# The row scales of the first norm go through DRAM instead of through TensorE

## The chip, the cores and the metric

The kernel runs on one core of a Trainium2 chip. The time is device microseconds of one launch. The kernel before takes 1110.6 us, the median of three runs (1110.36 to 1110.89).

## The reference

One hybrid decoder layer over 256 positions of width 1024, all in 32-bit floats: a mixer (8 mLSTM heads and 8 block-attention heads of 64), a mixture of 32 experts with 4 chosen for each position, and a gated per-layer embedding. What the change touches is the first norm and the combined projection behind it, with the gate columns of the mLSTM heads:

```
h = x * rsqrt(mean(x * x) + 1e-6) * mix_norm_g          # 256 rows, 1024 wide
u = h @ w_in                                            # 3600 columns, split among the head groups
ml_qk, ml_v, ml_o, ml_i, ml_f, mb_q, mb_k, mb_v = split(u)
i_pre = ml_i + igate_b ;  f_pre = ml_f + fgate_b        # 8 columns each: the gates
q_b = rmsnorm(mb_q, q_norm_g) / 8 ;  k_b = rmsnorm(mb_k, k_norm_g)
```

Behind it stand the two mixers, `x += mixed @ w_out`, the experts (`w_gate_up` of 32 x 1024 x 2048 and `w_down` of 32 x 1024 x 1024, read in full), and the embedding with its gate `w_ple_gate`.

## The kernel before, in words

The rows are two tiles of 128 positions (`tt` 0 and 1). `x` lies in the tile named arena, and TensorE transposes it so that the 1024 inputs lie on the partitions, in eight slices (`k`). The transposed slices are multiplied by `mix_norm_g` and stored in `rawT` (named big in the profile): ScalarE writes slices 0 to 3 (`raw_half`, L1787), VectorE slices 4 to 7 (L1329). `rawT` still lacks the norm's factor, one number for each position, the row scale `rstd`. ScalarE sums the squares and takes the root (`row_root`, L1794), VectorE takes the reciprocal (`rstd`, L1317) into two columns of `stat`, one number per partition.

The projection runs as 18 jobs, each of eight steps over `k` into one of two PSUM banks (hu 0 and 1). Jobs 0 and 1 are the attention queries of the two row tiles. They take `rawT`, without the scale, and the scale is applied afterwards, on the rows. All later jobs take `hT`, which is `rawT` times the row scale. There the positions lie along the free dimension, so the scale is needed as a row of 256 numbers on all 128 partitions. Before the change two matmuls make that row: `stat`'s column, broadcast, against the identity (L776) into PSUM bank hu 3. `scaled(tt)` (L1334) makes one half of `hT` with it.

The gates are computed apart: eight small matmuls (L783) over all of `rawT` give partial sums `gpart`, which VectorE copies and multiplies by the same row (L1346, L1348), and two matmuls (L794) add the partial sums. VectorE then runs ten gate steps on 8 partitions (L1392 to L1403), with an exponential and a logarithm on ScalarE between them. `normed_half(i)` (L1354) divides job i's result by its heads' norms. It stands before the gate steps for job 0 and behind them for job 1.

The order on each engine is that in which the code is written, and every engine runs its own list. Semaphores join the lists. TensorE's list at the start is: transposes, job 0, the two row matmuls, the gates' partial sums, eight small transposes of parameter rows (L788), two steps of job 1, the gate sums, six steps of job 1, job 2 (L714), four transposes of job 0's normalised result (L807, which wait for the tenth gate step), four small ones (L816), job 3. Job 2 waits for both halves of `hT` and for job 0's bank (`normed_half(0)`), job 3 for `normed_half(1)`.

The weights come on SyncE's DMA queue into a ring of eleven slots of up to 2 MB. The next transfer into a slot is issued when TensorE has finished with the slot's content. The small parameters come on ScalarE's queue (q10 in the profile). One such round trip through DRAM exists already: the row maxima of the mLSTM heads are stored by ScalarE (L1831) and loaded on all partitions by SyncE (L490).

Of the kernel before, what the change touches and what calls it, by code (L numbers as in the profile page):

```python
# [15 lines left out]
F32 = mybir.dt.float32  # L16
I32 = mybir.dt.int32
U32 = mybir.dt.uint32
ALU = mybir.AluOpType
# [3 lines left out]
P = 128  # L23
# [10 lines left out]
def hybrid_layer(nc, x, p, mix_norm_g, w_in, conv_w, conv_b, igate_b, fgate_b, mlstm_head_g, q_norm_g,  # L34
                 k_norm_g, w_out, ffn_norm_g, w_router, b_router, w_gate_up, b_gate_up, w_down, b_down,
                 ple_norm_g, w_ple_gate, w_ple_proj, out):
    S, D = x.shape[1:]
# [3 lines left out]
    K = D // P  # L41
    TT = S // P
# [58 lines left out]
    with ctx:  # L101
        def sb(name, shape, dt=F32):
            return ctx.enter_context(nc.sbuf_tensor(name, shape, dt))

        def sem(name):
            return ctx.enter_context(nc.semaphore(name))


        hu = ctx.enter_context(nc.psum_tensor("hu", [P, 4, NB], F32))
# [5 lines left out]
        ident = sb("ident", [P, P])  # L115
# [16 lines left out]
        early = arena[:, TT * D:]  # L132

        stat = sb("stat", [P, 64])
# [41 lines left out]
        gpart = num_xg[:, 0:S]  # L176
# [33 lines left out]

        zeros = early[:, 0:P]
        sq_junk = early[:, 2 * S:2 * S + D]

        const_ready = sem("const_ready")
        zero_ready = sem("zero_ready")
# [6 lines left out]
        first_loaded = sem("first_loaded")  # L222
        second_loaded = sem("second_loaded")
        third_loaded = sem("third_loaded")
        rowb_ps = sem("rowb_ps")
        small_loaded = sem("small_loaded")
        late_loaded = sem("late_loaded")
        wo_ps = sem("wo_ps")
# [7 lines left out]
        gpart_ready = sem("gpart_ready")  # L236
# [5 lines left out]
        rstd_ready = sem("rstd_ready")  # L242
# [111 lines left out]
        def slot(n, width, parts):  # L354

            return ring[:, PRE_SLOT[n], 0:parts * width].rearrange("p (k n) -> p k n", n=width)
# [43 lines left out]
        def final_slot(c, width, parts):  # L400

            return ring[:, SLOT_OF[POSITIONS + c], 0:parts * width].rearrange("p (k n) -> p k n", n=width)

        def last_of_chunk(j):
            return j + 1 == JOBS or JOB_CHUNK[j + 1] != JOB_CHUNK[j]

        def done_job(j, ins):

            ins.then_inc(chunk_done if last_of_chunk(j) else job_ps, 1)
# [30 lines left out]
        def fin_bank(q, lo, hi):  # L440

            return (po[:, 1, :] if lo else LAST_BANKS[q])[:, lo:hi]
# [7 lines left out]
            return buf[:, q // HALVES, (q % HALVES) * NB:(q % HALVES + 1) * NB]  # L450

        xt_d = nc.dram_tensor("xt_scratch", (P, TT, D), F32).ap()
        negm_d = nc.dram_tensor("negm_scratch", (H, S), F32).ap()

        block = ctx.enter_context(nc.Block())
# [230 lines left out]
        def _(pe):  # L686
            mm = nc.tensor.matmul
# [65 lines left out]
            def raw_job(tt, ks):  # L753

                for k in ks:
                    last = mm(hu[:, tt, :], rawT[:, k, tt * P:(tt + 1) * P], slot(0, NB, K)[:, k, :], start=(k == 0),  # L756
                              stop=(k == K - 1), skip_group_check=True)
                return last
# [12 lines left out]
            raw_transposes(1)  # L771
            wait_chunk(pe, 0)
            done_job(0, raw_job(0, range(6, K)))
            for tt in range(TT):
                pe.wait_ge(rstd_ready, tt + 1)
                last = mm(hu[:, 3, tt * P:(tt + 1) * P], stat[:, 16 + tt:17 + tt].to_broadcast([P, P]), ident[:], start=True, stop=True)  # L776
            last.then_inc(rowb_ps, 1)
            pe.wait_ge(hT_act, 8)
            pe.wait_ge(hT_dve, 2)
            pe.wait_ge(small_loaded, 16 * 3)  # L780
            for k in range(K):
                c = 32 * (k % 4)
                last = mm(aux[c:c + 32, 1, 0:S], w_if[:, k, :], rawT[:, k, :], start=(k < 4), stop=(k >= 4),  # L783
                          skip_group_check=True)
            last.then_inc(gpart_ps, 1)
            pe.wait_ge(rows_loaded, 16 * 8)
            for k in range(K):
                last = tr(hu[:, 2, k * ROWS:(k + 1) * ROWS], rows[:, k * P:(k + 1) * P], ident[0:ROWS, 0:ROWS])  # L788
            last.then_inc(cols_ps, 1)
            raw_job(1, range(0, 2))  # L790
            pe.wait_ge(gpart_ready, 2)
            pe.wait_ge(const_ready, 6)
            for gi in range(2):
                last = mm(aux[0:H, 0, gi * S:(gi + 1) * S], sel_part[:, gi * H:(gi + 1) * H], gpart, start=True, stop=True)  # L794
            last.then_inc(gate_ps, 1)
            done_job(1, raw_job(1, range(2, K)))

            def norm_transposes(i):

# [14 lines left out]
            for c, src in enumerate((arow, negmt)):  # L814
                for tt in range(TT):
                    last = tr(hu[:, 2 + c, tt * H:(tt + 1) * H], src[:, tt * P:(tt + 1) * P], ident[0:H, 0:H])  # L816
# [228 lines left out]
            def scatter_expert(q, e, bank, more=False):  # L1045

                tt, n = divmod(q, HALVES)
                r = slice(n * SLOTS, (n + 1) * SLOTS)
                return mm(bank, ghotT[r, e, tt * P:(tt + 1) * P], out_s[e][r, :], start=(e == 0), stop=(e == 1 and not more))  # L1049
# [80 lines left out]
            with pe.Fori(0, npass) as ps:  # L1130
# [151 lines left out]
                for tt in range(TT):  # L1282
                    for n in range(HALVES):
                        last = scatter_expert(HALVES * tt + n, 1, LAST_BANKS[HALVES * tt + n])
# [9 lines left out]
            for q, lo, hi in FIN:  # L1294
                tt, n = divmod(q, HALVES)
                for k in range(K):
# [4 lines left out]
                    elif n == 0:  # L1301
                        pe.wait_ge(hT_dve, 2 + 4 * tt + k - 3)
                    last = mm(fin_bank(q, lo, hi), x3T[:, k, tt * P:(tt + 1) * P],  # L1303
                              final_slot(k // 4, D, 4)[:, k % 4, n * NB + lo:n * NB + hi],
                              start=(k == 0), stop=(k == K - 1))
# [6 lines left out]
        def _(dve):  # L1312
            v = nc.vector
# [20 lines left out]
            def scaled(tt):  # L1334

                r = slice(tt * P, (tt + 1) * P)
                dve.wait_ge(hT_act, 4 * tt + 4)
                dve.wait_ge(hT_dve, tt + 1)
                v.tensor_tensor(hT[:, :, r], rawT[:, :, r],
                                hu[:, 3, r].rearrange("p (o t) -> p o t", o=1).to_broadcast([P, K, P]), ALU.mult)\  # L1340
                 .then_inc(xs_ready, 1)

            dve.wait_ge(rowb_ps, 1)
            scaled(0)
            dve.wait_ge(gpart_ps, 1)
            v.tensor_copy(gpart, aux[:, 1, 0:S]).then_inc(gpart_ready, 1)  # L1346
            dve.wait_ge(gpart_ready, 1)
            v.tensor_tensor(gpart, gpart, hu[:, 3, 0:S], ALU.mult).then_inc(gpart_ready, 1)  # L1348
            dve.wait_ge(cols_ps, 1)
            v.tensor_copy(cols[:].rearrange("p k r -> p (k r)"), hu[:, 2, 0:K * ROWS]).then_inc(cols_ready, 1)  # L1350
            scaled(1)
            dve.wait_ge(cols_ready, 1)

            def normed_half(i):  # L1354

                ss = small[:, 0:H]
                dve.wait_ge(sq_ready, i + 1)
                v.tensor_reduce(ss, sq_junk[:, i % 2 * W:(i % 2 + 1) * W].rearrange("p (h d) -> p h d", h=H), AX.X, ALU.add).then_inc(nstat, 1)
                dve.wait_ge(nroot, i + 1)
                v.reciprocal(small[:, 3 * H:4 * H], small[:, 2 * H:3 * H]).then_inc(nstat, 1)  # L1360
                dve.wait_ge(nstat, 2 * i + 2)
                if i >= 2:
                    dve.wait_ge(normT_ps, i - 1)
                out = normed[:, i % 2, :].rearrange("p (h d) -> p h d", h=H)
                q = hu[:, i % 2, :].rearrange("p (h d) -> p h d", h=H)
                inv = small[:, 3 * H:4 * H].rearrange("p (h o) -> p h o", o=1).to_broadcast([P, H, DH])
                if i < TT:
                    v.scalar_tensor_tensor(out=out, in0=q, scalar=stat[:, 16 + i:17 + i], in1=inv, op0=ALU.mult, op1=ALU.mult)\
                     .then_inc(normed_ready, 1)
                else:  # L1370
                    v.tensor_tensor(out, q, inv, ALU.mult).then_inc(normed_ready, 1)
# [13 lines left out]
            n = [0]  # L1385
# [378 lines left out]
        def _(act):  # L1764
            a = nc.scalar

            def root(i, src, wait):

                if wait:
                    act.wait_ge(sum_ready, i - 1)  # L1770
                a.activation(stat[:, 8 + i:9 + i], src, ACT.Sqrt, scale=1.0 / D, bias=eps_t[:]).then_inc(root_ready, 1)
# [15 lines left out]
            def raw_half(tt):  # L1787

                act.wait_ge(xT_ps, 2 * tt + 1)
                for k in range(4):  # L1790
                    a.activation(rawT[:, k, tt * P:(tt + 1) * P], QUAD_BANKS[2 * tt][:, k * P:(k + 1) * P], ACT.Copy,
                                 scale=g_mix[:, k:k + 1]).then_inc(hT_act, 1)

            def row_root(tt):  # L1794

                act.wait_ge(x_loaded[tt], 16)
                if tt:
                    act.wait_ge(ss_ready, tt)
                a.activation(sq_junk[:], xt[:, tt, :], ACT.Square, accum_out=stat[:, tt:tt + 1]).then_inc(ss_ready, 1)
                act.wait_ge(ss_ready, tt + 1)  # L1800
                root(tt, stat[:, tt:tt + 1], False)
# [2 lines left out]
            raw_half(0)  # L1804
            row_root(0)
            row_root(1)
            raw_half(1)
            act.wait_ge(root_warm, 1)

            for i in range(4):  # L1810
# [248 lines left out]
            for i, (q, lo, hi) in enumerate(FIN):  # L2059
                tt = q // HALVES  # L2060
# [27 lines left out]
```

## Time and profile before

| | before |
|---|---|
| median of 3 runs | 1110.6 us |
| the profiled execution | 1110.49 us |
| its span | 1108.7 us |
| TensorE busy | 1071.0 us, 97% |
| weights and the rest moved | 431.89 MB, 390 GB/s on average |

A row of the timeline gives the start, the duration, the engine (PE is TensorE, DVE VectorE, ACT ScalarE, SPq and ACTq the issuing of a DMA by SyncE and ScalarE), the line, the operation, the tiles written and read, the shapes, and in brackets how long the engine had been idle and for what. The chain of waits is followed back from the last instruction. A row of it is a stretch that the end depended on. "PEclk" is the granted TensorE clock, 1.00 being 2.4 GHz and 0.50 being 1.2 GHz.

### The profile page before, as it was taken

To read this page: it belongs to the slowest core of one execution; us is meant where nothing else is said; L and a number is where in the kernel's file an instruction comes from. 1 tells how busy PE (TensorE), PEld (TensorE's weight loads), DVE (VectorE), ACT (ScalarE), POOL (GpSimd) and SP (SyncE) were. 2 spreads that over 40 slices of the span, in tenths; PEclk is the share of its full clock that TensorE was granted. 3 is DMA by queue.
4 is the path that set the end of the run, shared out by engine and by line. 5 is a ranking of instruction groups with operands and counts; after the bars stand their busy time and mean duration, and the time that the engine had idled before them with its cause. 6 is when DMAs were issued, how large, how long until landed. Compare 5 with 4: busy or idle time off the path is not lost.

```text
span 1108.7 us, 12040 instructions
## 1 busy us (share of the span) xinstructions
PE 1071.0 (97%) x5136; PEld 445.1 (40%) x5136; DVE 258.7 (23%) x534; ACT 144.6 (13%) x283; POOL 16.3 (1%) x40
## 2 busy tenths in 40 slices
PE   9999999999999999999999899998989999999898
PEld 5485563434343434343434232333333344423234
DVE  4274242231121212121212121111212021202122
ACT  4134341100000000000000000000000100000022
POOL 1001100000000000000000000000000000000000
PEclk9999999999999999999999999999999999999999
DMA  9943589999999999999999999999999999999971
GB/s 347 361 168 123 240 343 387 426 426 430 427 426 429 427 427 427 427 429 425 428 429 426 429 429 426 429 427 427 427 427 425 429 427 426 429 428 426 427 324 38
DMA packets 43004, 431.89 MB, mean 390 GB/s; under 512 B 6231, under 2 KB 6751, under 8 KB 17606
## 3 DMA queue, kind: packets, MB, share of 16 engines
q1 hardware_dynamic: 42736, 431.07, 93.0%
q8 instruction: 41, 0.67, 0.2%
q14 instruction: 13, 0.11, 0.0%
q10 hardware_dynamic: 214, 0.04, 0.0%
HBM read 430.04 MB, written 1.06 MB: 389 GB/s over the span
## 4 chain that ended last, share of the span: by engine, by line
PE 66%; DMA 33%; DVE 0%; issue 0%; ACT 0%; SPq 0%; DVEq 0%; ACTq 0%
PE hu L1094 23%; DMA ring<-in_w_gate_up 23%; PE po L1124 14%; DMA ring<-in_w_down 6%; PE aux L1041 5%; PE hu L714 5%; DMA ring<-in_w_ple_gate 3%; PE hu L720 3%; PE aux L1049 2%; PE hu L1086 2%; PE hu L730 2%; PE hu L756 1%; PE po L1101 1%; PE aux L1303 1%; PE aux L1074 1%; PE po L1303 1%
## 5 line engine op out<-in xcount | busy, mean ns | idle before, releaser
L1094 PE MATMUL hu<-ring,num_xg 128*64 128x512 f32 x1920 | 433.2, 598 | 24.4 <-DMA ring<-in_w_gate_up 24.4
L1094 PEld LDWEIGHTS hu<-ring,num_xg 128*64 128x64 f32 x1920 | 131.9, 137 | 305.9 <-issue 258.7
L1124 PE MATMUL po<-ring,arena 128*64 128x512 f32 x976 | 217.8, 596 | 6.5 <-DMA ring<-in_w_down 6.5
L1124 PEld LDWEIGHTS po<-ring,arena 128*64 128x64 f32 x976 | 67.4, 137 | 152.7 <-issue 136.8
L1669 DVE TENSOR_SCALAR arena<-hu 128x512 f32<-128x512 f32 x31 | 21.4, 692 | 431.9 <-PE hu L1094 431.9
L1645 DVE TENSOR_TENSOR arena<-arena,aux 128x512 f32<-128x512 f32 x58 | 37.3, 684 | 133.2 <-PE aux L1049 121.4
L1041 PEld LDWEIGHTS aux<-num_xg,big 128*128 128x128 f32 x512 | 58.4, 192 | 13.0 <-issue 13.0
L1041 PE MATMUL aux<-num_xg,big 128*128 128x128 f32 x512 | 61.4, 278 | 0.0
L714 PE MATMUL hu<-ring 128*128 128x512 f32 x128 | 56.7, 596 | 0.0
L1992 ACT ACTIVATE hu<-arena 128x512 f32<-128x512 f32 x31 | 18.6, 601 | 250.7 <-DVE arena L1669 250.7
L1658 DVE TENSOR_SCALAR arena<-iota_s,posm,gates 128x128 f32<-128x128 f32 x64 | 17.9, 343 | 118.3 <-PE po L1124 115.3
L2008 ACT COPY arena<-po 128x512 f32<-128x512 f32 x16 | 9.4, 586 | 220.7 <-PE po L1114 220.7
L1049 PE MATMUL aux<-num_xg,arena 64*128 64x512 f32 x124 | 35.0, 641 | 0.1
L714 PEld LDWEIGHTS hu<-ring 128*128 128x128 f32 x128 | 23.8, 190 | 27.7 <-issue 27.4
L1086 PE MATMUL hu<-bias,sel_part 32*64 32x512 f32 x256 | 34.8, 612 | 0.0
L1049 PE MATMUL aux<-arena 64*128 64x512 f32 x124 | 31.8, 589 | 0.0
L1996 ACT COPY arena<-po 128x512 f32<-128x512 f32 x31 | 18.2, 586 | 90.3 <-PE po L1101 90.3
L720 PE MATMUL hu<-ring 128*128 128x256 f32 x128 | 29.5, 385 | 0.0
L1094 PE MATMUL hu<-ring,arena 128*64 128x512 f32 x128 | 28.1, 594 | 0.1
L730 PE MATMUL hu<-ring 128*128 128x512 f32 (+1 forms) x64 | 25.8, 543 | 0.0
L720 PEld LDWEIGHTS hu<-ring 128*128 128x128 f32 x128 | 23.7, 190 | 4.8 <-DVE ring L1444 1.0
L2000 ACT COPY num_xg<-po 128x512 f32<-128x512 f32 x16 | 9.4, 586 | 114.9 <-PE po L1124 114.9
(276 smaller groups left out, 606.8 us busy)
## 6 DMA issues: line engine op xcount, KB each, us to landing
ring<-in_w_gate_up SPq DMA_DIRECT2D x125, 2048.0 KB, 37.3
ring<-in_w_down SPq DMA_DIRECT2D x60, 2048.0 KB, 38.0
ring<-in_w_in SPq DMA_DIRECT2D x6, 2048.0 KB, 17.1
ring<-in_w_gate_up SPq DMA_DIRECT2D x6, 1024.0 KB, 7.9
ring<-in_w_out SPq DMA_DIRECT2D x2, 2048.0 KB, 11.7
ring<-in_w_down SPq DMA_DIRECT2D x4, 1024.0 KB, 37.1
ring<-in_w_ple_gate SPq DMA_DIRECT2D x2, 2048.0 KB, 33.6
ring<-in_w_in SPq DMA_DIRECT2D x4, 512.0 KB, 6.6
```

The lines of the kernel that those rows point to most:

```text
L714: last = mm(bank, hT[:, k, tt * P:(tt + 1) * P], slot(n, NB, K)[:, k, :], start=(k == 0), stop=(k == K - 1))
L720: last = mm(bank[:, 0:S], slot(n, NB, K)[:, k, ct * P:(ct + 1) * P], hT[:, k, :], start=(k == 0), stop=(k == K - 1))
L730: last = mm(bank[:, lo:hi], mixT[:, k, tt * P:(tt + 1) * P], slot(n, D, 4)[:, k % 4, b * NB + lo:b * NB + hi], start=(k == 4), stop=(k == 3))
L1041: last = mm(bank[:, (k % 4) * P:(k % 4 + 1) * P], h2[:, tt, k * P:(k + 1) * P], onehot[:, tt, :, :].rearrange("p e s -> p (e s)"), start=( ...
L1049: return mm(bank, ghotT[r, e, tt * P:(tt + 1) * P], out_s[e][r, :], start=(e == 0), stop=(e == 1 and not more))
L1086: mm(hu[n * SLOTS:(n + 1) * SLOTS, 2 * e + b, :], expert_rows(b, expert), bias[32 * b:32 * b + E, n * NB:(n + 1) * NB], start=first, stop= ...
L1094: last = mm(hu[n * SLOTS:(n + 1) * SLOTS, 2 * e + b, :], rows_of[:, k, e * SLOTS:(e + 1) * SLOTS], w[:, o:o + NB], start=first, stop=(k == ...
L1124: last = mm(bank[n * SLOTS:(n + 1) * SLOTS, :], actT[:, f, h * SLOTS:(h + 1) * SLOTS], w[:, o:o + NB], start=(h == 0 and f == 0), stop=(h ...
L1303: last = mm(fin_bank(q, lo, hi), x3T[:, k, tt * P:(tt + 1) * P], final_slot(k // 4, D, 4)[:, k % 4, n * NB + lo:n * NB + hi], start=(k == ...
L1645: v.tensor_tensor(quad(xt, q), quad(xt, q), banks[q], ALU.add).then_inc(y_done, 1)
L1669: v.tensor_scalar(glu, hu[:, 2 * e, :], LIMIT, None, ALU.min).then_inc(glu_ready, 1)
L1992: a.activation(hu[:, 2 * e, :], gated(2 * pair + e), ACT.Sigmoid, scale=ALPHA).then_inc(sig_ready, 1)
```

## The change

The two matmuls that made the row are gone. ScalarE stores the two columns of scales as 2 x 128 numbers in a DRAM tensor, and loads the 256 numbers back on all 128 partitions into `scales`, a part of arena. The stores stand before `raw_half(1)` in ScalarE's list and wait for both reciprocals. The load stands behind it and waits for both stores to have landed. In TensorE's list the gate sums move from behind two steps of job 1 to behind four. In VectorE's list the copies out of PSUM come first, then the gates' product, then both halves of `hT`.

```diff
             done_job(0, raw_job(0, range(6, K)))
-            for tt in range(TT):
-                pe.wait_ge(rstd_ready, tt + 1)
-                last = mm(hu[:, 3, tt * P:(tt + 1) * P], stat[:, 16 + tt:17 + tt].to_broadcast([P, P]), ident[:], start=True, stop=True)
-            last.then_inc(rowb_ps, 1)
             pe.wait_ge(hT_act, 8)
 ...
-            raw_job(1, range(0, 2))
+            raw_job(1, range(0, 4))
             pe.wait_ge(gpart_ready, 2)
 ...
-            done_job(1, raw_job(1, range(2, K)))
+            done_job(1, raw_job(1, range(4, K)))
 ...
                 v.tensor_tensor(hT[:, :, r], rawT[:, :, r],
-                                hu[:, 3, r].rearrange("p (o t) -> p o t", o=1).to_broadcast([P, K, P]), ALU.mult)\
+                                scales[:, r].rearrange("p (o t) -> p o t", o=1).to_broadcast([P, K, P]), ALU.mult)\
                  .then_inc(xs_ready, 1)
 
-            dve.wait_ge(rowb_ps, 1)
-            scaled(0)
             dve.wait_ge(gpart_ps, 1)
             v.tensor_copy(gpart, aux[:, 1, 0:S]).then_inc(gpart_ready, 1)
-            dve.wait_ge(gpart_ready, 1)
-            v.tensor_tensor(gpart, gpart, hu[:, 3, 0:S], ALU.mult).then_inc(gpart_ready, 1)
             dve.wait_ge(cols_ps, 1)
             v.tensor_copy(cols[:].rearrange("p k r -> p (k r)"), hu[:, 2, 0:K * ROWS]).then_inc(cols_ready, 1)
-            scaled(1)
             dve.wait_ge(cols_ready, 1)
+            dve.wait_ge(scales_loaded, 16)
+            dve.wait_ge(gpart_ready, 1)
+            v.tensor_tensor(gpart, gpart, scales, ALU.mult).then_inc(gpart_ready, 1)
+            for tt in range(TT):
+                scaled(tt)
 ...
             row_root(1)
+            act.wait_ge(rstd_ready, TT)
+            for tt in range(TT):
+                act.dma_start(scale_d[tt:tt + 1, :].rearrange("o p -> p o"), stat[:, 16 + tt:17 + tt]).then_inc(scales_stored, 16)
             raw_half(1)
+            act.wait_ge(scales_stored, 16 * TT)
+            act.dma_start(scales, scale_d.rearrange("t p -> (t p)").rearrange("(o n) -> o n", o=1).to_broadcast([P, S]))\
+               .then_inc(scales_loaded, 16)
```

TensorE's list before, from job 0 to job 2 (L756 are the steps of jobs 0 and 1, L776 the row matmuls, L783 the gates' partial sums, L794 the gate sums):

```order
L749 MATMUL po<-ident,arena 128x128 x8
L756 MATMUL hu<-ring,big 128x512 x2
L776 MATMUL hu<-ident,stat 128x128 x2
L783 MATMUL aux<-big,ring 32x256 x8
L788 MATMUL hu<-ident,ring 128x10 x8
L756 MATMUL hu<-ring,big 128x512 x2
L794 MATMUL aux<-num_xg,sel_part 8x256 x2
L756 MATMUL hu<-ring,big 128x512 x6
L714 MATMUL hu<-ring 128x512 x8
```

The same place after the change, three to nine lines further down in the file:

```order
L752 MATMUL po<-ident,arena 128x128 x8
L759 MATMUL hu<-ring,big 128x512 x2
L782 MATMUL aux<-big,ring 32x256 x8
L787 MATMUL hu<-ident,ring 128x10 x8
L759 MATMUL hu<-ring,big 128x512 x4
L793 MATMUL aux<-num_xg,sel_part 8x256 x2
L759 MATMUL hu<-ring,big 128x512 x4
L717 MATMUL hu<-ring 128x512 x8
```

The row matmuls are gone, and two steps of job 1 have moved ahead of the gate sums.

ScalarE's list before, from the second root on (`raw_half(1)`, then the squares of job 0 and their root):

```order
L1799 ACTIVATE arena,stat<-arena 128x1024
L1771 ACTIVATE stat<-stat,eps_t 128x1
L1791 ACTIVATE big<-po,g_mix 128x128 x4
L1819 ACTIVATE arena<-hu,stat 128x512
L1823 ACTIVATE small<-small,eps_t 128x8
```

The same place after:

```order
L1798 ACTIVATE arena,stat<-arena 128x1024
L1770 ACTIVATE stat<-stat,eps_t 128x1
L1808 DMA scale_scratch<-stat 128x1 x2
L1790 ACTIVATE big<-po,g_mix 128x128 x4
L1811 DMA arena<-scale_scratch 128x256
L1824 ACTIVATE arena<-hu,stat 128x512
L1828 ACTIVATE small<-small,eps_t 128x8
```

Two stores stand ahead of `raw_half(1)` now, and a load ahead of the squares of job 0.

VectorE's list before, from the second reciprocal to the first gate step (L1339 are the halves of `hT`):

```order
L1320 RECIPROCAL stat<-stat 128x1
L1339 TENSOR_TENSOR ring<-big,hu 128x8x128
L1346 COPY num_xg<-aux 128x256
L1348 TENSOR_TENSOR num_xg<-num_xg,hu 128x256
L1350 COPY cols<-hu 128x80
L1339 TENSOR_TENSOR ring<-big,hu 128x8x128
L1358 TENSOR_REDUCE small<-arena 128x8
L1360 RECIPROCAL small<-small 128x8
L1368 SCALAR_TENSOR_TENSOR ring<-hu,stat,small 128x512
L1392 TENSOR_SCALAR ring<-aux,fg_bias 8x256
```

The same place after:

```order
L1319 RECIPROCAL stat<-stat 128x1
L1343 COPY num_xg<-aux 128x256
L1345 COPY cols<-hu 128x80
L1349 TENSOR_TENSOR num_xg<-num_xg,arena 128x256
L1338 TENSOR_TENSOR ring<-big,arena 128x8x128 x2
L1357 TENSOR_REDUCE small<-arena 128x8
L1359 RECIPROCAL small<-small 128x8
L1367 SCALAR_TENSOR_TENSOR ring<-hu,stat,small 128x512
L1391 TENSOR_SCALAR ring<-aux,fg_bias 8x256
```

Everything from the gates' product on now stands behind the load of the scales.

## Rows read from the trace of the kernel before

**Rows 1.** The page: engines, then the span in 40 slices.
```profile
PE 1071.0 (97%) x5136; PEld 445.1 (40%) x5136; DVE 258.7 (23%) x534; ACT 144.6 (13%) x283; POOL 16.3 (1%) x40
PEclk9999999999999999999999999999999999999999
DMA  9943589999999999999999999999999999999971
```

**Rows 2.** The chain of waits: start, duration, what it was.
```profile
12.52 1.72 PE hu L756 x4
14.69 1.00 PE aux L783 x16
16.28 1.91 PE hu L756 x4
18.20 0.96 PE aux L794 x4
19.16 5.35 PE hu L756 x12
24.51 6.87 PE hu L714 x16
32.15 7.06 PE hu L714 x16
...
543.18 39.89 DMA ring<-in_w_gate_up
```

**Rows 3.** Stretches: bounds, length, busy PE PEld DVE ACT POOL, clock, DMA share, GB/s.
```profile
12.00:16.00 4.00, 4.00 (x35) 2.34 (x34) 1.98 (x4) 1.83 (x5) 0.00 (x0) 1.00 1.05 387
142.00:144.00 2.00, 2.00 (x10) 1.55 (x10) 0.69 (x1) 0.16 (x1) 1.60 (x2) 1.00 0.12 45
157.00:160.00 3.00, 3.00 (x19) 2.67 (x18) 1.65 (x8) 2.69 (x4) 0.00 (x0) 1.00 0.57 186
200.00:543.00 343.00, 342.93 (x1728) 131.94 (x1726) 74.32 (x129) 26.58 (x45) 0.00 (x0) 1.00 1.01 428
```

**Rows 4.** The timeline around the row matmuls.
```profile
12.11 1.14 ACT L1791 ACTIVATE big<-po,g_mix 128x128 f32<-128x128 f32 x4 [0.23 <-PE po L749]
13.24 0.15 DVE L1320 RECIPROCAL stat<-stat 128x1 f32<-128x1 f32 x1
```

**Rows 5.** DMAs on ScalarE's queue: two issues, and its packets in 44.8:45.5.
```profile
0.80 0.42 ACTq L1773 DMA_DIRECT2D g_mix<-in_mix_norm_g  x1
...
41.07 0.28 ACTq L1831 DMA_DIRECT2D negm_scratch<-arena  x1
...
q10 hardware_dynamic: 16, 0.01, 4.0%
```

**Rows 6.** Packets on SyncE's queue in 12:16, and DMAs to landing (last number).
```profile
q1 hardware_dynamic: 755, 1.55, 105.0%
...
g_mix<-in_mix_norm_g ACTq DMA_DIRECT2D x1, 4.0 KB, 4.1
ring<-in_mlstm_head_g SPq DMA_DIRECT2D x1, 256.0 KB, 9.1
```

**Rows 7.** The timeline of VectorE from the gates' product to `normed_half(1)`.
```profile
16.37 0.42 DVE L1348 TENSOR_TENSOR num_xg<-num_xg,hu 128x256 f32<-128x256 f32 x1
16.71 0.23 DVE L1350 COPY cols<-hu 128x80 f32<-128x80 f32 x1
16.86 1.21 DVE L1339 TENSOR_TENSOR ring<-big,hu 128x1024 f32<-128x1024 f32 x1
17.99 0.68 DVE L1358 TENSOR_REDUCE small<-arena 128x8 f32<-128x512 f32 x1
...
27.88 0.75 DVE L1368 SCALAR_TENSOR_TENSOR ring<-hu,stat,small 128x512 f32<-128x512 f32 x1
```

**Rows 8.** Stretches around a fall of the clock, columns as in rows 3.
```profile
809.80:813.40 3.60, 3.60 (x16) 1.05 (x16) 0.00 (x0) 0.00 (x0) 0.00 (x0) 1.00 1.03 437
813.45:815.90 2.45, 0.00 (x1) 0.00 (x0) 0.00 (x0) 0.00 (x0) 0.00 (x0) 1.00 1.01 421
816.80:820.20 3.40, 3.40 (x10) 0.96 (x8) 0.00 (x0) 0.00 (x0) 0.00 (x0) 0.50 0.98 419
```

**Rows 9.** A shorter idle stretch in the timeline, and what followed in the chain.
```profile
583.11 1.08 PE L1094 MATMUL hu<-ring,num_xg 128*64 128x512 f32 x4 [1.24 <-DMA ring<-in_w_gate_up]
...
583.11 3.65 PE hu L1094 x16
```

More of the change, by code:

```diff
@@ L212, in hybrid_layer @@
         sq_junk = early[:, 2 * S:2 * S + D]
+        scales = early[:, 6 * S:7 * S]
         const_ready = sem("const_ready")
@@ L224, in hybrid_layer @@
         third_loaded = sem("third_loaded")
-        rowb_ps = sem("rowb_ps")
+        scales_stored = sem("scales_stored")
+        scales_loaded = sem("scales_loaded")
         small_loaded = sem("small_loaded")
@@ L452, in hybrid_layer @@
         xt_d = nc.dram_tensor("xt_scratch", (P, TT, D), F32).ap()
+        scale_d = nc.dram_tensor("scale_scratch", (TT, P), F32).ap()
         negm_d = nc.dram_tensor("negm_scratch", (H, S), F32).ap()
```

## The prediction

> **What bounds the kernel now.** I read the page first: TensorE is busy 97% of the span and the DMA engines nearly all of it from the fifth slice on [rows 1]. Both are candidates, so the place decides. The chain of waits says that from 12 us to 543 us the end depends on TensorE, and that at 543 us it changes over to a transfer of weights, 39.89 us from issue to landing [rows 2]. Around the change TensorE has no gap at all: 4.00 us busy of the 4.00 from 12 us on [rows 3]. So whatever TensorE waits there is added to its list in full.
>
> Does that reach the end, since behind 543 us the transfers set the pace? The stream of weights has full engines from 200 us (share 1.01), but not at 142 us (0.12) and not at 157 us (0.57) [rows 3]. There it waits for ring slots that TensorE has to free, while TensorE is busy throughout. A later TensorE frees them later, the stream starts its unbroken run later, and the whole rest moves by the same amount. I pass every microsecond of the front on to the end, one to one.
>
> **The change, part by part.**
>
> *The two row matmuls go.* In the chain there are 0.45 us between the end of job 0 (12.52 + 1.72 = 14.24) and the partial sums (14.69) [rows 2]. That is a gain of 0.45 us, if the partial sums can start at 14.24.
>
> *They cannot, because `raw_half(1)` is late.* The partial sums read all of `rawT`, and before, ScalarE had its four slices written at 12.11 + 1.14 = 13.25 [rows 4], well hidden. Now ScalarE first waits for the second reciprocal, which ends at 13.24 + 0.15 = 13.39 [rows 4], and issues two DMAs. The nearest row for one of 128 partitions is 0.42 us of issuing [rows 5]. With 0.1 us for the semaphore: stores issued at 13.5 and 13.92, ScalarE free at 14.35, `raw_half(1)` done at 15.5. The partial sums start near 15.6 instead of 14.69, so this alone turns the gain of 0.45 into a loss of about 0.9 us. They and the small transposes take 16.28 - 14.69 = 1.59, the four steps of job 1 twice the 1.92 of two (18.20 - 16.28) [rows 2]: TensorE stands before the gate sums at 21.0.
>
> *When do the scales arrive?* Call it T. Two transfers in a row, each waited for. The best row is the store that the kernel already makes on the same queue, beside the same stream of weights: issued at 41.07, all of its 16 packets (8 rows and what closes them) moved between 44.8 and 45.5 [rows 5]. So some 4.3 us from issue to landing, nearly all of it before the first byte. Ours has 128 pieces, eight on each of 16 DMA engines. If each takes its turn with one packet of the weights, of which 755 went by in 4 us on 16 engines [rows 6], 4 x 16 / 755 = 0.085 us each, seven more pieces cost 0.6 us, and the other store's pieces stand in between. I take 5.1 us from the second issue: 13.92 + 5.1 = 19.0. The load is issued at 19.1. It has the same 4.3 us, 0.6 us for eight turns, and its pieces are 1 KB each, about half of those 0.085 us, 0.35 us for eight: 5.3 us, so T = 24.4. From below: g_mix, 128 pieces of 32 bytes issued into an empty chip, took 4.1 us to land [rows 6]; 13.92 + 4.1 + 0.1 + 4.1 gives T = 22.2. A gain from a transfer is not possible, since the scales were there at once before. From above: a load on all partitions, of 256 KB on the other queue, took 9.1 us [rows 6], which with a store of 5.1 gives T = 28.2. I take 24.4, since its rows are of the same queue under the same traffic.
>
> *What waits for T on VectorE.* The gates' product, both halves of `hT`, `normed_half(0)`, the ten gate steps and `normed_half(1)` are all behind it. From the spacing of the starts: product 16.71 - 16.37 = 0.34, each half of `hT` 17.99 - 16.86 = 1.13 [rows 7]. So the reduction of `normed_half(0)` starts at T + 0.1 + 0.34 + 2.26 = T + 2.7. From there to the end of `normed_half(1)` it was 27.88 + 0.75 - 17.99 = 10.64 us [rows 7], through ScalarE's roots, exponential and logarithm, which keep their place in that sequence. That is T + 13.35, and job 3 can start at T + 13.45.
>
> *What waits for T on TensorE.* The gate sums start at T + 0.65 (semaphore, 0.42 for the product, semaphore, weight load). For T = 24.4 that is 25.05, so TensorE idles for 4 us. Then 0.96 for the sums, four steps at 5.35 x 4 / 6 = 3.57, and 32.15 - 24.51 = 7.64 from the start of job 2 to that of job 3 [rows 2]: T + 12.8. VectorE's path is the later one, at T + 13.45. The two moved steps of job 1 cover 2 x 0.96 = 1.9 us of the wait, and the calculation has them in it. Job 2 itself needs both halves and job 0's bank, T + 4.75, and TensorE comes at T + 5.2. The transposes need the tenth gate step, about 2.1 us before T + 13.35, that is T + 11.3, and TensorE comes at T + 12.05.
>
> *The clock.* Behind 2.45 us in which TensorE did nothing, the granted clock was 0.50 (1.2 of 2.4 GHz) for 3.40 us of work [rows 8], and behind 1.24 us of idling another stretch kept its rate: 16 matmuls in 3.65 us [rows 9], against 3.60 at full clock and 10 in 3.40 in the slow stretch [rows 8]. Our gap is 4 us, so I expect one such stretch here. It costs half of 3.4, 1.7 us, on TensorE's path: T + 14.5, which is then the later of the two.
>
> *The rest.* ScalarE stands at the store's wait until 19.1, and the squares of job 0 behind it come near 20 instead of 14.33; their reader on VectorE is at T + 2.7 anyway. GpSimd's and SyncE's later waits for the gate steps feed work far behind. The scales read from arena instead of PSUM I price at nothing: both products run one element per cycle by their durations (1.21 us for 1024) [rows 7], and a change of 0.1 us there either way is inside the range. The three DMAs move 128 KB and 1 KB, some 0.35 us of the engines at 387 GB/s [rows 3], in front of weights whose first unmet need is at 543 us [rows 2]: nothing.
>
> *The sum.* Before, job 3 started at 32.15 [rows 2]. After: 24.4 + 14.5 = 38.9. That is 6.75 us later, or 24.4 + 13.45 - 32.15 = 5.7 us if the clock stays up. The profiled execution took 1110.49 us (0.1 below the median), so I forecast 1110.5 + 6.75 = 1117.25, rounded to 1117.2.
>
> **The rivals.**
>
> *Quick round trip.* If T is below about 19.7, VectorE's path (T + 13.45) is behind TensorE's own, which stands before the gate sums at 21.0 and reaches job 3 at 21.0 + 0.96 + 3.57 + 7.64 = 33.2. Then only the late `raw_half(1)` counts: +1.0 us, 1111.5. It needs both transfers within about 2.8 us of issue. For it: 1 KB and less to move. Against: the shortest landing in the rows is 4.1 us [rows 6]. The Trainium skill (DMA: Bandwidth & Descriptors, Anatomy of one DMA) gives 2.0 us of fixed cost for each DMA and next to nothing for so few bytes, which by that page puts T near 18.9 and the result in this rival; no row of this trace shows a transfer that short.
>
> *Not slower at all.* The same with the store's issue costing ScalarE next to nothing, so that `raw_half(1)` is done by 14.2: it would need issues of 0.1 us or less each against the 0.28 and 0.42 of the rows [rows 5]. Then the 0.45 us of the row matmuls are won: 1110.0. It decides from T below 18.2.
>
> *The delay is swallowed.* TensorE's first wait for weights is at 543 us [rows 2]. If the stream did not start later, TensorE could be 7 us late in front and lose nothing: 1110.5. Against it speak the two stretches in which the stream has nothing to do [rows 3].
>
> *A slow load or slow stores.* 4-byte writes to DRAM do not occur in this trace. If the pair takes as long as the upper bound, T = 28.2, then 28.2 + 14.5 - 32.15 = 10.55 us: 1121.0.
>
> **Chances.** The forecast's own case (T from 22.2 to 26.5) 73%, the slow transfers 13%, quick round trip 7%, swallowed delay 5%, not slower at all 2%. The range goes from T = 22.2 without a fall of the clock (3.5 us: 1114.0), half a microsecond taken off for the estimates in it, to just above the upper bound: 1113.5 to 1121.5. About 0.2%, 2.2 us, is what a measurement of this kernel can tell from no change. Slower by more than that: 0.86, the first two cases. Within: 0.11, quick, swallowed and not slower in most of their cases. Faster: 0.03.
>
> **What would show it.** In the profile after: two stores issued near 13.5 on ScalarE's queue, `raw_half(1)` starting near 14.4; the load issued near 19; the gates' product on VectorE starting near 24.5; an idle TensorE before the gate sums, about 4 us, where there was none; a stretch at clock 0.50 behind it; job 3 starting near 39; and the same lateness of 6 to 7 us at the first expert matmul and at the end. It is wrong if the gate sums do not wait (quick round trip), or if the late start of job 3 is not found again at the end (swallowed).

## The result and the profile after

| | before | after |
|---|---|---|
| median of 6 runs each | 1110.48 us | 1127.35 us |
| range of the runs | 1109.78 to 1110.91 | 1126.65 to 1128.99 |
| ratio, 95% interval | | 1.0151 (1.0141 to 1.0161) |
| span of the profiled execution | 1108.7 us | 1124.9 us |

The kernel is slower by 16.9 us. Forecast were 6.7, with a range that ended at 1121.5. The direction was right, the size less than half of what came.

The chain of waits of the changed kernel says where it went (start, duration, what). It answers to [rows 2]:

```profile
13.73 12.58 DMA scale_scratch<-stat
26.33 7.13 DMA arena<-scale_scratch
34.02 1.88 PE aux L793 x4
35.90 4.89 PE hu L759 x8
40.79 6.87 PE hu L717 x16
48.44 7.06 PE hu L717 x16
```

The second store alone took 12.58 us, the load 7.13. Job 3 (the last row, L717 is L714 of before) starts at 48.44 instead of 32.15, 16.3 us late. The span has grown by 16.2. So nearly all of it arose before job 3, and nearly all of it reached the end.

The timeline around it (start, duration, engine, line, in brackets the idle time before). These rows answer to [rows 4, 7]:

```profile
13.33 0.85 ACTq L1808 DMA_DIRECT2D scale_scratch<-stat  x2
14.23 1.14 ACT L1790 ACTIVATE big<-po,g_mix 128x128 f32<-128x128 f32 x4 [2.52 <-DVE stat L1319]
15.43 0.85 PE L782 MATMUL aux<-big,ring 128*32 128x256 f32 x12 [1.27 <-ACT big L1790]
...
33.54 0.43 DVE L1349 TENSOR_TENSOR num_xg<-num_xg,arena 128x256 f32<-128x256 f32 x1 [16.16 <-DMA arena<-scale_scratch]
34.02 1.88 PE L793 MATMUL aux<-num_xg,sel_part 128*8 128x256 f32 x4 [13.30 <-DVE num_xg L1349]
```

ScalarE issues both stores and is late for `raw_half(1)`, and TensorE waits 1.27 us for it, as forecast. The last two rows are the trip through DRAM: VectorE had nothing to do for 16.16 us, TensorE for 13.30.

Stretches of the changed kernel, columns as in [rows 3]:

```profile
12.00:16.00 4.00, 2.73 (x20) 1.25 (x23) 0.76 (x2) 1.14 (x4) 0.00 (x0) 1.00 1.05 386
19.00:21.00 2.00, 1.72 (x5) 0.42 (x3) 0.00 (x0) 0.00 (x0) 0.00 (x0) 1.00 1.04 27
20.80:34.00 13.20, 0.00 (x0) 0.00 (x0) 0.46 (x2) 0.69 (x1) 0.00 (x0) 0.65 0.97 216
34.10:38.30 4.20, 4.20 (x7) 1.47 (x8) 3.80 (x6) 1.42 (x2) 0.00 (x0) 0.50 1.05 400
158.00:161.00 3.00, 3.00 (x13) 2.19 (x12) 1.30 (x4) 0.30 (x1) 1.62 (x2) 1.00 0.18 76
216.00:560.00 344.00, 343.94 (x1730) 132.35 (x1728) 74.75 (x131) 27.08 (x46) 0.00 (x0) 1.00 1.01 427
```

Three things stand here. From 19 to 21 us the DMA engines are as busy as ever (1.04) and move 27 GB/s instead of 387: the stores hinder the weights too. Behind the gap TensorE works at the lower clock, a granted clock of 0.50. And 16 us further down the stream of weights has the same hole as before (0.18 at 158 us) and the same unbroken run behind it: the whole rest has moved.

The packets of SyncE's queue between 18 and 22 us (number, MB, share of 16 engines) answer to [rows 6]:

```profile
q1 hardware_dynamic: 145, 0.30, 113.5%
```

That is 1.135 x 16 x 4 / 145 = 0.50 us for a packet of the weights, of some 2 KB. Before it was 1.050 x 16 x 4 / 755 = 0.089 us.

### The profile page after: what moved, and what is told of

Same layout as the page of the kernel before. It is cut to its first block, busy times and chain, and to the rows that moved or that the text cites. A ratio compares the mean times of both kernels' runs of the same rounds, so it can differ in the third digit from the quotient of the medians.

```text
span 1124.9 us, 12035 instructions
## 1 busy us (share of the span) xinstructions
PE 1071.4 (95%) x5132; PEld 444.6 (40%) x5132; DVE 258.6 (23%) x534; ACT 144.4 (13%) x283; POOL 16.4 (1%) x40
## 4 chain that ended last, share of the span: by engine, by line
PE 65%; DMA 34%; DVE 1%; issue 0%; ACT 0%; SPq 0%; ACTq 0%; DVEq 0%
PE hu L1093 22%; DMA ring<-in_w_gate_up 22%; PE po L1123 14%; DMA ring<-in_w_down 6%; PE aux L1040 5%; PE hu L717 5%; DMA ring<-in_w_ple_gate 3%; PE hu L723 3%; PE aux L1048 2%; PE hu L1085 2%; PE hu L733 2%; DMA scale_scratch<-stat 1%; PE po L1100 1%; PE aux L1302 1%; PE hu L759 1%; PE aux L1073 1%
## 5 line engine op out<-in xcount | busy, mean ns | idle before, releaser
L717 PE MATMUL hu<-ring 128*128 128x512 f32 x128 | 56.7, 596 | 0.0
L717 PEld LDWEIGHTS hu<-ring 128*128 128x128 f32 x128 | 23.8, 190 | 27.7 <-issue 27.4
```

The costliest lines, as they stand in the source:

```text
L717: last = mm(bank, hT[:, k, tt * P:(tt + 1) * P], slot(n, NB, K)[:, k, :], start=(k == 0), stop=(k == K - 1))
```

## The experiments

Theory A, formed on this trace: many 4-byte pieces written side by side into 1 KB of DRAM hinder each other and all that the DMA engines do besides. The rivals are these: any small piece is slow; a store to DRAM under this traffic is slow whatever its shape; the wait and the blocked issues around the stores make them slow; and the new order on VectorE and TensorE costs as well. In the edits below, "..." stands for lines left out, such as the declarations of semaphores and of the DRAM tensor.

### The stores alone

The two stores are added to the kernel before, in the place where the changed kernel has them. Nothing on the path waits for them:

```diff
...
             row_root(1)
+            act.wait_ge(rstd_ready, TT)
+            for tt in range(TT):
+                act.dma_start(scale_d[tt:tt + 1, :].rearrange("o p -> p o"), stat[:, 16 + tt:17 + tt]).then_inc(scales_stored, 16)
             raw_half(1)
...
+            pool.wait_ge(scales_stored, 16 * TT)
+            g.memset(stat[:, 60:61], 0.0)
             pool.wait_ge(gate_step, GATE_STEPS)
```

> The kernel before, with the two stores of 128 x 4 bytes put where the changed kernel has them; nobody on the path waits for them (GpSimd alone does, and then writes one idle column). Theory A, the 4-byte writes to DRAM themselves choke the DMA engines: the weights fall below 100 GB/s for some 5 us from 17 to 24 us, the stores land some 12 us after issue, as in the changed kernel, and the time moves only by the late raw_half(1), +0.8 us. Rival B, the stores are slow because ScalarE then sits in a wait and SyncE in a blocked issue, not by themselves: landing in 5 us, weights undisturbed. Rival C, the disturbance delays the weights enough to cost time by itself: over +3 us with no wait for the scales.

Measured: 1111.99 us beside 1110.86 (1.0008, 0.9998 to 1.0017). Its landing, shortest, median and longest of the two, and a stretch:

```profile
DMA to landing us min/median/max: 12.4/12.7/13.1
```
```profile
19.00:21.00 2.00, 2.00 (x7) 0.76 (x7) 1.60 (x4) 1.35 (x2) 0.00 (x0) 1.00 1.33 21
```

The stores are as slow with ScalarE at work instead of waiting, so that half of rival B falls. The other half, SyncE's blocked issue, is still there: it stands in the kernel before as well (one group of issues takes 21.30 us from 4.64 on, here 28.13), and the next run decides on it. The weights choke just as much (21 GB/s), and the time hardly moves. Up to 60 us the chain of waits of this run holds TensorE alone and no transfer of weights, so these are far enough ahead here, and rival C falls too. What costs is waiting for the stores, not having them.

### The pieces apart

```diff
-        scale_d = nc.dram_tensor("scale_scratch", (TT, P), F32).ap()
+        scale_d = nc.dram_tensor("scale_scratch", (TT, P, 1024), F32).ap()
...
-                act.dma_start(scale_d[tt:tt + 1, :].rearrange("o p -> p o"), stat[:, 16 + tt:17 + tt]).then_inc(scales_stored, 16)
+                act.dma_start(scale_d[tt, :, 0:1], stat[:, 16 + tt:17 + tt], allow_slow_non_contiguous=True).then_inc(scales_stored, 16)
```

> As the run with the stores alone, but each 4-byte piece goes to its own 4 KB of DRAM instead of beside its neighbours. If neighbouring pieces in the same line of memory hinder each other, the landing falls from 12 us to 5 or 6 us and the weights keep about 387 GB/s. If any 4-byte write to DRAM is slow, both stay as with the pieces together.

```profile
DMA to landing us min/median/max: 5.2/5.4/5.7
```
```profile
19.00:21.00 2.00, 2.00 (x8) 0.82 (x8) 1.60 (x4) 1.55 (x2) 0.10 (x1) 1.00 1.05 390
```

The same 256 pieces of 4 bytes, on the same queue at the same moment, land in 5.4 us, and the weights keep 390 GB/s. (Time 1112.1 us, 1.0012, 1.0002 to 1.0021.) SyncE's issue is blocked here for 21.16 us, as in the kernel before, so the rest of rival B falls. It is the neighbourhood, not the size or the number.

How near is too near? The same was run with 64 and with 512 bytes from piece to piece (the last size 16 and 128 instead of 1024), and with pieces of 512 bytes one behind the other:

> As the run with the stores alone, each 4-byte piece 64 bytes from the next. My theory (pieces hinder each other only where they fall into the same small stretch of DRAM) leaves open how long the stretch is. If it is 64 bytes or less: landing near 5.4 us, weights undisturbed, as at 4 KB. If it is longer: landing between 5.4 and 12.7 us with a dip in the weights.

> The same with 512 bytes between pieces. If the stretch is 512 bytes or less: landing near 5.4 us, weights at 385 GB/s. If only the number of pieces per page or bank counts: still slow.

```diff
-                act.dma_start(scale_d[tt, :, 0:1], stat[:, 16 + tt:17 + tt], allow_slow_non_contiguous=True).then_inc(scales_stored, 16)
+                act.dma_start(scale_d[tt], xt[:, tt, 0:P]).then_inc(scales_stored, 16)
```

> The stores alone, with 2 x 128 pieces of 512 bytes (a part of x) in place of 4 bytes, one behind the other in DRAM. If neighbours as such were the trouble, this would be slow too. If it is several partial writes to one stretch: landing near 6 us (more bytes, 128 KB), and no dip beyond the 0.3 us that the bytes take.

The landings, for 64 bytes:

```profile
DMA to landing us min/median/max: 5.5/6.0/6.4
```

for 512 bytes:

```profile
DMA to landing us min/median/max: 5.1/5.4/5.7
```

and for the wide pieces:

```profile
DMA to landing us min/median/max: 5.2/5.5/5.7
```

The weights kept 389 GB/s or more from 19 to 21 us in all three; the times of the one run each were 1111.46, 1111.39 and 1111.55 us. At 64 bytes the trouble is gone but for half a microsecond of landing (and 379 GB/s from 17 to 19 us). So it takes several small pieces within 64 bytes or less. Which smaller stretch decides was not tried.

### To a column on chip

```diff
-                act.dma_start(scale_d[tt:tt + 1, :].rearrange("o p -> p o"), stat[:, 16 + tt:17 + tt]).then_inc(scales_stored, 16)
+                act.dma_start(stat[:, 58 + tt:59 + tt], stat[:, 16 + tt:17 + tt]).then_inc(scales_stored, 16)
```

> As the run with the stores alone, but the same 2 x 128 pieces of 4 bytes go to two idle columns on chip instead of to DRAM. If it is the number of small pieces (reading, descriptors), landing stays near 12 us. If it is writing to DRAM, landing is near 5 us and the weights keep 387 GB/s. Time +0.8 us in both.

Measured: 1112.78 us (1.0017, 1.0008 to 1.0027), and from 19 to 21 us 382 GB/s. The stores stand in the list of DMAs as `stat<-stat`, with the median of the two landings at the end:

```profile
stat<-stat ACTq DMA_DIRECT2D x2, 0.5 KB, 5.7
```

So the same 256 pieces of 4 bytes, side by side in two columns on chip, land in 5.7 us, and the weights do not choke: they had 364 GB/s at the least, from 17 to 19 us. It takes writes to DRAM to make them slow. The run cost 0.8 us more than the one with the stores to DRAM alone; its two issues took 0.53 and 0.61 us instead of 0.36 and 0.45, which makes `raw_half(1)` start later behind them by a third of a microsecond, and the rest is inside the intervals.

### The stores in a quiet stream

The changed kernel, with the weights held back:

```diff
             for n in range(1, len(SECTIONS)):
+                if n == 2:
+                    sp.wait_ge(scales_loaded, 16)
                 load(n, slot(n, NB, K), w_in_k[:, :, SECTIONS[n]:SECTIONS[n] + NB])
...
```

> The changed kernel, with SyncE holding back the weights from the third block on until the scales are loaded, so that the trip meets no other traffic. If the stores are slow by themselves (pieces against each other in DRAM): landing still near 12 us, T near 31. If they are slow only beside the weights: landing 3 to 5 us, T = 21 to 23, and the time falls to +4 to +6 us over the kernel before, unless the held back weights then come late themselves.

Measured: 1119.93 us beside 1110.78 (1.0085, 1.0068 to 1.0102). The chain, the packets of ScalarE's queue from 16.0 to 17.4 us, and a stretch behind them:

```profile
13.85 8.78 DMA scale_scratch<-stat
22.65 4.14 DMA arena<-scale_scratch
q10 hardware_dynamic: 288, 0.00, 11.6%
19.00:21.00 2.00, 1.83 (x5) 0.52 (x3) 0.00 (x0) 0.00 (x0) 0.00 (x0) 1.00 0.00 0
```

All 288 packets of the stores (256 pieces and what closes them) moved between 16.0 and 17.4 us, the first of them beside the last of the weights. From 17.4 to 22.6 nothing moved on any queue. What passes in these 5 us the trace does not show; writes that are not yet confirmed would be one reading. So the stores are slow by themselves (8.78 us), and slower beside the weights (12.58). I had expected either the one or the other; it is both. The load takes 4.14 us in quiet and 7.13 in the changed kernel.

### Two rows of 512 bytes instead of 256 pieces

TensorE first turns the two columns into two rows, and one store takes these to DRAM:

```diff
...
             done_job(0, raw_job(0, range(6, K)))
+            pe.wait_ge(rstd_ready, TT)
+            tr(hu[0:TT, 3, 0:P], stat[:, 16:16 + TT], ident[:]).then_inc(rowb_ps, 1)
...
+            dve.wait_ge(rowb_ps, 1)
+            v.tensor_copy(scales[0:TT, 0:P], hu[0:TT, 3, 0:P]).then_inc(row_copied, 1)
             dve.wait_ge(gpart_ps, 1)
...
-            act.wait_ge(rstd_ready, TT)
-            for tt in range(TT):
-                act.dma_start(scale_d[tt:tt + 1, :].rearrange("o p -> p o"), stat[:, 16 + tt:17 + tt]).then_inc(scales_stored, 16)
             raw_half(1)
-            act.wait_ge(scales_stored, 16 * TT)
+            act.wait_ge(row_copied, 1)
+            act.dma_start(scale_d, scales[0:TT, 0:P]).then_inc(scales_stored, 16)
+            act.wait_ge(scales_stored, 16)
...
```

> The changed kernel, but TensorE first transposes the two columns of scales to two rows (one small matmul), VectorE copies them, and one store of 2 x 512 bytes replaces the two stores of 128 x 4 bytes; raw_half(1) is ahead of it again. If the 4-byte writes are what is slow: landing in some 4.5 us, load issued near 19, scales there at T = 24.5, time T - 17.6 = +6.9 us, 1117.4. If any trip through DRAM under this traffic is slow (12 us for a store): no better than the changed kernel, 1127.

Measured: 1118.0 us beside 1110.78 (1.0069, 1.0053 to 1.0086). The chain:

```profile
14.78 4.30 DMA scale_scratch<-arena
19.10 5.45 DMA arena<-scale_scratch
25.12 1.87 PE aux L797 x4
26.99 4.64 PE hu L761 x8
31.63 6.87 PE hu L719 x16
39.28 7.06 PE hu L719 x16
```

This comes near the forecast's sum: a store of 4.30 us (forecast 4.3 before the surcharge for pieces), a load of 5.45 (5.3), the scales at 24.55 (24.4), job 3 at 39.28 (38.9), the time 7.2 us over before (6.7). That the scales come when forecast is in part chance: this store is issued 0.86 us later than the forecast's second one, and lands in 0.8 us less than the 5.1 of the forecast. A trip through DRAM under this traffic costs about 10 us, and some 9.4 us of the changed kernel's loss went with the shape of its stores (1127.35 - 1118.0; the kernel before had medians of 1110.5 and 1110.8 beside them).

### Half the pieces

One store of 128 x 8 bytes. The scales of the two row tiles then alternate, and VectorE reads them in steps of two (not shown here):

```diff
...
-        scale_d = nc.dram_tensor("scale_scratch", (TT, P), F32).ap()
+        scale_d = nc.dram_tensor("scale_scratch", (P, TT), F32).ap()
...
-            for tt in range(TT):
-                act.dma_start(scale_d[tt:tt + 1, :].rearrange("o p -> p o"), stat[:, 16 + tt:17 + tt]).then_inc(scales_stored, 16)
+            act.dma_start(scale_d, stat[:, 16:16 + TT]).then_inc(scales_stored, 16)
...
```

> The changed kernel with one store of 128 x 8 bytes instead of two of 128 x 4 bytes (half the pieces, the same bytes). If the cost goes with the number of pieces: the store lands in half of the 12.6 us plus a fixed part, 8 to 9 us, and the time is 3 to 5 us below the changed kernel. If it goes with the fact of partial writes at all, or with the bytes: as the changed kernel.

```profile
13.43 6.63 DMA scale_scratch<-stat
20.08 6.18 DMA arena<-scale_scratch
```

Measured: 1120.48 us (1.0092, 1.0074 to 1.011), 6.9 us under the changed kernel. Expected were 3 to 5 us less and a landing of 8 to 9; both guesses were too cautious. The weights kept 338 GB/s from 17 to 19 us and 357 from 19 to 21. Over the 5.4 us of undisturbed pieces, 256 pieces of 4 bytes cost 7.2 us more and 128 pieces of 8 bytes 1.2. The cost does not go in proportion to the pieces. Their number, their size and the number of stores changed together here, so which of them decides is open.

### The clock

`keep_warm(bank, n)` makes TensorE transpose the identity n times into a bank whose content nobody reads. First try, on the changed kernel:

```diff
             raw_job(1, range(0, 4))
+            keep_warm(hu[:, 3, :], 92)
```

> The changed kernel, with 92 transposes of the identity into an unused bank (12 us of idle work on TensorE) in front of the wait for the gates' product. If the low clock costs what the trace says (4.4 us of work at half rate, of which VectorE's path hides about half): 1.0 to 1.2 us less than the changed kernel, TensorE full clock behind the gap. Rival: the clock is not on the path, since VectorE's chain sets job 3: no difference.

```profile
21.00:31.00 10.00, 10.00 (x92) 9.88 (x91) 0.00 (x0) 0.69 (x1) 0.00 (x0) 1.00 1.03 150
31.40:35.10 3.70, 0.00 (x0) 0.00 (x0) 0.43 (x2) 0.00 (x0) 0.00 (x0) 0.89 0.99 354
35.20:41.00 5.80, 5.80 (x9) 2.17 (x10) 5.07 (x9) 2.08 (x4) 0.00 (x0) 0.50 1.05 395
```

Measured: 1128.44 us (1.0157, 1.014 to 1.0174): a failed experiment. The idle work lasted 10.2 us instead of the 12 counted on and ran out at 31.3 us, the product came 1.1 us later in this execution than in the changed kernel's (34.67 against 33.54), and 3.7 us of idling brought the clock down all the same. Second try, where the gap is short and known, on the kernel with the two rows:

```diff
             raw_job(1, range(0, 4))
+            keep_warm(po[:, 0, :], 44)
```

> The kernel with one store of two rows of 512 bytes, and 44 transposes of the identity into an idle bank (4.9 us at the 0.111 us of the earlier run) in the 5.5 us in which TensorE waits for the gates' product. If the low clock is on the path as worked out, the clock stays at 1.00 and VectorE's chain is what sets job 3, at T + 13.45 = 38.0 instead of 39.3: 1.2 us less than that kernel, 1116.8 beside a kernel before of 1110.8. Rival: VectorE's chain set job 3 already, and nothing changes (1118.0).

Measured: 1117.26 us beside 1110.81 (1.0059, 1.0045 to 1.0072). A stretch of that kernel behind the gap, VectorE's product, the gate sums and job 3:

```profile
25.50:29.00 3.50, 2.81 (x9) 1.17 (x10) 3.29 (x4) 0.00 (x0) 0.00 (x0) 1.00 1.05 387
25.71 0.43 DVE L1356 TENSOR_TENSOR num_xg<-num_xg,arena 128x256 f32<-128x256 f32 x1 [9.20 <-DMA arena<-scale_scratch]
...
26.19 1.03 PE L798 MATMUL aux<-num_xg,sel_part 128*8 128x256 f32 x4 [1.52 <-DVE num_xg L1356]
...
39.02 7.13 PE L719 MATMUL hu<-ring 128*128 128x512 f32 x16 [0.53 <-DVE ring L1374]
```

and of the one without the idle work:

```profile
25.20:28.90 3.70, 3.70 (x7) 1.24 (x7) 3.30 (x5) 0.92 (x2) 0.00 (x0) 0.50 1.06 389
24.64 0.43 DVE L1355 TENSOR_TENSOR num_xg<-num_xg,arena 128x256 f32<-128x256 f32 x1 [8.40 <-DMA arena<-scale_scratch]
...
39.20 7.13 PE L719 MATMUL hu<-ring 128*128 128x512 f32 x16
```

From product to job 3 it is 13.3 us with the clock at 1.00 and 14.6 with it down, and in the first TensorE then waits for VectorE's chain (0.53 <-DVE), in the second it does not. VectorE's chain was not what set job 3 already, which was the rival. The 1.2 us that were worked out are there in the trace. The medians differ by 0.7 us only, within their intervals, and the load in the profiled execution took 6.2 us here against 5.5.

### The new order without the trip

The row matmuls back, everything else of the change kept:

```diff
...
-        scales = early[:, 6 * S:7 * S]
+        scales = hu[:, 3, 0:S]
...
+            for tt in range(TT):
+                pe.wait_ge(rstd_ready, tt + 1)
+                last = mm(hu[:, 3, tt * P:(tt + 1) * P], stat[:, 16 + tt:17 + tt].to_broadcast([P, P]), ident[:], start=True, stop=True)
+            last.then_inc(rowb_ps, 1)
...
-            dve.wait_ge(scales_loaded, 16)
+            dve.wait_ge(rowb_ps, 1)
...
```

(The stores and the load are gone too.)

> The changed kernel with the two row matmuls put back in place of the trip through DRAM: VectorE's new order and the gate sums behind four steps stay. My theory: the trip is the whole loss, so this runs as before, within 0.3 us (1110.2 to 1110.8). Rival: the new order costs by itself, since both halves of hT and normed_half(0) come in front of the gate steps and the gate sums come 1.9 us later: +1 us or more.

Measured: 1110.39 us beside 1110.86 (0.9999, 0.999 to 1.0008). The order costs nothing and wins nothing that can be told. The trip, with the late `raw_half(1)` that its stores bring, is the whole loss, and no version here beats the kernel before by more than the noise.

## Why the prediction was off, step by step

- **TensorE's delay passes on to the end, one to one: right.** Job 3 16.3 us late, the span 16.2. The stream's hole at 142 us is at 158 us, the unbroken run behind it as before.
- **The row matmuls' 0.45 us are lost to the late `raw_half(1)`: right.** It starts at 14.23 (forecast 14.35), and the partial sums at 15.43 (15.6). With the stores alone the kernel is 1.1 us slower by its medians.
- **The landing of the stores, "5.1 us from the second issue": this term failed.** It measured 12.58. Of the sum's error of 9.5 us up to job 3 it makes 7.5. I had taken the row of eight pieces of 1 KB, and priced 128 pieces by their turns at the engines alone. The turns were about right: the same pieces apart land in 5.4 us, side by side on chip in 5.7. What was missing is what small pieces side by side do to each other in DRAM. The trace had no such write, the prediction said so, and its bound from above was taken from a load all the same. A bound for an operation that no row shows should not have been a load's.
- **The load, 5.3 us: 1.8 us too low.** It took 7.13 in the changed kernel, 5.45 and 6.2 beside undisturbed weights (the two kernels with rows), 4.14 with almost no weights beside it. So one part of the excess comes without any choke. That it is longest behind the choked stores is seen in these rows; by what path, no run tells. The kernel before has a load of the same form, of the row maxima back on all partitions (L490, on SyncE's queue), which the prediction does not weigh. It moves 1 MB instead of 128 KB and landed in 8.6 us. The difference in bytes at the 387 GB/s of [rows 3] is 2.4 us, so an estimate from this row would have been 6.2 us, nearer to what came than 5.3.
- **The two paths from T to job 3: right.** At full clock 13.3 us from product to job 3 (forecast T + 13.45, the product at T + 0.1), on VectorE's side as worked out; with the lower clock 14.6 (14.4) and on TensorE's side.
- **The clock falls and costs about 1 us: right in kind.** It was at 0.50 for 4.2 us of work (the row from 34.1 to 38.3) instead of the 3.4 of [rows 8]; product to job 3 14.9 us, half a microsecond more than forecast. 7.5 + 1.8 + 0.5, less 0.2 for the store issued earlier, is 9.6, against 9.5 measured.
- **The rivals.** The quick trip is refuted: even in quiet the load took 4.14 us, and the kindest store 4.30. (The "1 KB and less to move" that spoke for it is the stores and one piece of the load; the load as a whole moves 128 KB, as the prediction says elsewhere.) The 2.0 us of the Trainium skill (DMA: Bandwidth & Descriptors, Anatomy of one DMA) spoke for that rival too, but that section is about DMAs issued by GpSimd, and these are issued by ScalarE. No run here shows a DMA of ScalarE's that lands within 2.0 us; the shortest landing is the 4.1 us of [rows 6]. The swallowed delay is refuted by the end. "Slow stores" was the right rival, priced with T = 28.2, where T came out at 33.5.

On the cause the Trainium skill has a rule (DMA: Bandwidth & Descriptors, Specifications): below 512 bytes a transfer is a read-modify-write. The runs agree in part. Four bytes at a distance of 64 bytes are far below 512 and cost little (6.0 us and 389 GB/s); 4 bytes side by side take 12.7 us. So the small size alone is not the price. That several DMA engines modify the same short stretch in turn would explain it, and explain the 5 us of silence in the quiet run; this is argued from that rule and not shown. What the runs show is the condition: several small pieces within less than 64 bytes, written to DRAM.

## What to carry to other kernels

A column that lies along the partitions should not be stored to neighbouring addresses in DRAM in 4-byte pieces: it took 12.6 us to land and cut the weights beside it to 27 GB/s, where two rows of 512 bytes took 4.3. Turning the column on TensorE first is worth a small matmul. Where TensorE has no time, pieces 64 bytes apart landed in 6.0 us; reading them back from there was not tried. Doing the whole job on TensorE, as before, cost 0.45 us. A dependent store and load through DRAM costs about 10 us here even in its best shape; it needs that much cover in front of every reader, and four steps of 0.9 us are not it.

## What was not expected of the hardware

- 256 four-byte writes side by side hold up the traffic of other queues: a 2 KB packet of the weights took 0.50 us on average instead of 0.089, while the share of busy DMA engines read 1.04. Only the 27 GB/s beside it tell that hardly anything moved.
- The time between the last packet and the landing can be the larger part: 5 us of 8.8 in the quiet run. In the changed kernel too the stores' last packet had moved by 22 us, and they landed at 26.3.
- An idle gap of 3.7 us behind 10 us of transposes brought the granted clock down to 0.50 (the failed experiment). A gap of 1.52 us, with TensorE busy without a gap before it, did not (1.00 behind it, in the kernel with two rows and idle work), and in the kernel before 2.45 us had been enough [rows 8].
